# Reordering the products inside each k tile of a decoder layer, so that neighbouring matmuls write different PSUM banks

## The reference, cut to what matters

```python
h = rmsnorm(x, g_mix)
proj = h @ w_in                      # q, k, v, index and gate columns
out_a = dsa_sparse_attention(...)    # 64 of 256 keys by an indexer
out_b = forgetting_attention(...)
mixed = sigmoid(gate_a) * (out_a @ w_o_a) + sigmoid(gate_b) * (out_b @ w_o_b)
x = x + mixed @ w_out
h = rmsnorm(x, g_ffn)
x = x + (silu(h @ w_ffn_gate) * (h @ w_ffn_up)) @ w_ffn_down      # D_FF = 5632
h = rmsnorm(x, g_ple)
x = x + sigmoid(h @ w_ple_gate) * (p @ w_ple_proj)
out = rmsnorm(x, g_final)
```

## Time and profile before

| | |
|---|---|
| runs timed | 1548.62, 1548.97, 1549.17 us |
| median | 1548.97 us |
| span of the profiled execution | 1546.9 us |
| outside of the span (median less span) | 2.1 us |
| TensorE matmul busy | 1516.1 us, 98% of the span |
| mean granted TensorE clock | 0.993 of full speed |
| moved by DMA | 277.56 MB, 179 GB/s |

### The profile page before, as it was taken

The page is one execution under the profiler, slowest core; times in us unless marked ns, Lnnn a source line. Parts: engine busy times, 40 slices in busy tenths (PEclk is TensorE's granted clock), DMA queues, the critical chain, the costliest instruction groups (busy, mean ns, idle before and its releaser), DMA issues.

```text
span 1546.9 us, 25491 instructions
## 1 busy us (share of the span) xinstructions
PE 1516.1 (98%) x8805; PEld 1326.9 (86%) x8805; DVE 986.6 (64%) x1194; ACT 742.2 (48%) x967; POOL 126.4 (8%) x175
## 2 busy tenths in 40 slices
PE   5999999999999999999999999999999999999997
PEld 4888998888988888888888888888888888888886
DVE  6965676667656776766666566556555455555765
ACT  6544435544444664454444444444444444444554
POOL 4011101100111000220000000000000001000031
PEclk8999999999999999999999999999999999999998
DMA  5665475555655555566555655656565565556553
GB/s 140 202 182 174 145 236 164 162 171 177 181 162 163 186 193 182 175 192 188 182 186 176 199 181 182 196 179 188 177 194 174 189 200 177 193 190 198 168 164 109
DMA packets 278124, 277.56 MB, mean 179 GB/s; under 512 B 13048, under 2 KB 275648, under 8 KB 277696
## 3 DMA queue, kind: packets, MB, share of 16 engines
q1 hardware_dynamic: 277632, 275.78, 57.1%
q10 hardware_dynamic: 448, 1.19, 0.2%
HBM read 274.83 MB, written 2.11 MB: 179 GB/s over the span
## 4 chain that ended last, share of the span: by engine, by line
PE 96%; DVE 2%; DMA 1%; ACT 0%; issue 0%; POOL 0%; ACTq 0%; DVEq 0%
PE acc L1178 54%; PE acc L1179 28%; PE acc L1176 3%; PE acc L1175 2%; PE side L1178 2%; PE acc L1280 1%; PE acc L1279 1%; PE acc L1278 1%; PE side L1179 1%; DVE hn L779 1%; DMA rope_c<-in_rope_rows 1%; PE side L1291 0%; PE side L1297 0%; DVE ls L723 0%; PE side L1176 0%
## 5 line engine op out<-in xcount | busy, mean ns | idle before, releaser
L723 DVE TENSOR_TENSOR ls<-ws,hs 128x1024 fp32r<-128x1024 f32 (+2 forms) x528 | 642.9, 1232 | 436.5 <-ACT hs L418 431.9
L418 ACT ACTIVATE hs<-ws 128x1024 fp32r<-128x1024 f32 (+2 forms) x528 | 542.3, 1040 | 535.7 <-PE acc L1179 304.6
L1178 PE MATMUL acc<-xg,hs 128*128 128x512 f32 x1560 | 556.5, 399 | 0.6 <-DVE y_ple L1095 0.6
L1179 PE MATMUL acc<-xg,ls 128*128 128x256 f32 x1560 | 438.1, 281 | 0.0
L1178 PE MATMUL acc<-hn,hs 128*128 128x512 f32 x1005 | 366.4, 406 | 5.8 <-DVE hn L779 5.8
L1178 PEld LDWEIGHTS acc<-xg,hs 128*128 128x128 f32 x1560 | 293.1, 188 | 68.0 <-DVE y_ple L1095 1.0
L1179 PEld LDWEIGHTS acc<-xg,ls 128*128 128x128 f32 x1560 | 294.7, 189 | 5.0
L1179 PE MATMUL acc<-hn,ls 128*128 128x256 f32 x1005 | 283.6, 282 | 0.0
L1178 PE MATMUL acc<-ff,hs 128*128 128x512 f32 x688 | 239.9, 392 | 0.0
L1178 PEld LDWEIGHTS acc<-hn,hs 128*128 128x128 f32 x1005 | 190.5, 190 | 50.9 <-DVE hn L779 7.6
L1179 PEld LDWEIGHTS acc<-hn,ls 128*128 128x128 f32 x1005 | 191.5, 191 | 2.7
(11 more groups left out here) (258 smaller groups left out, 1464.9 us busy)
## 6 DMA issues: line engine op xcount, KB each, us to landing
ws<-in_w_in SPq DMA_DIRECT2D x152, 512.0 KB, 3.7
ws<-in_w_ffn_gate SPq DMA_DIRECT2D x88, 512.0 KB, 4.6
ws<-in_w_ffn_up SPq DMA_DIRECT2D x88, 512.0 KB, 4.4
ws<-in_w_ffn_down SPq DMA_DIRECT2D x64, 512.0 KB, 3.5
ws<-in_w_out SPq DMA_DIRECT2D x32, 512.0 KB, 4.3
ws<-in_w_ple_gate SPq DMA_DIRECT2D x32, 512.0 KB, 4.6
ws<-in_w_ffn_down SPq DMA_DIRECT2D x32, 384.0 KB, 3.6
ws<-in_w_o_b SPq DMA_DIRECT2D x16, 512.0 KB, 3.6
```

The costliest lines, as they stand in the source:

```text
L418: act.activation(hs[:, j, 0:n], ws[:, j, 0:n], ACT.Copy).then_inc(h_split, 1)
L723: dve.tensor_tensor(ls[:, j, 0:n], ws[:, j, 0:n], hs[:, j, 0:n].bitcast(F32), ALU.subtract).then_inc(l_split, 1)
L1178: pe.matmul(whole, *high, start=begins, stop=False)
L1179: mm = pe.matmul(half, *low, start=False, stop=False)
```

## The change

Inside `consume` the loops over rows and k tiles change places: for two rows at a time, and for each k tile, first the high products of both rows, then the low products of both rows. In the last k tile of a unit the two low products come first and then the two high ones. Where only one row is worked on (the first unit, and the last PLE unit), the order is as before. In the PLE projection with its four rows, the rows go two by two.

```diff
-            for m in range(banks) if tile is None else (tile,):
+            rows = range(banks) if tile is None else (tile,)
+            for at_row in range(0, len(rows), 2):
                 for q, k in enumerate(tiles):
-                    at = slice(q * width + m * P, q * width + (m + 1) * P)
                     begins, ends = first and q == 0, last and q == len(tiles) - 1
-                    high, low = (hs[:, j, at], src[:, k, :]), (ls[:, j, at], src[:, k, 0:TOK])
-                    whole, half = acc_of(bank + m, 2 * TOK), acc_of(bank + m, TOK)
-                    if ends:
-                        pe.matmul(half, *low, start=False, stop=False)
-                        mm = pe.matmul(whole, *high, start=False, stop=True)
-                    else:
-                        pe.matmul(whole, *high, start=begins, stop=False)
-                        mm = pe.matmul(half, *low, start=False, stop=False)
+
+                    def whole(m):
+                        at = slice(q * width + m * P, q * width + (m + 1) * P)
+                        return pe.matmul(acc_of(bank + m, 2 * TOK), hs[:, j, at], src[:, k, :], start=begins, stop=ends)
+
+                    def half(m):
+                        at = slice(q * width + m * P, q * width + (m + 1) * P)
+                        return pe.matmul(acc_of(bank + m, TOK), ls[:, j, at], src[:, k, 0:TOK], start=False, stop=False)
+
+                    for part in (half, whole) if ends else (whole, half):
+                        for m in rows[at_row:at_row + 2]:
+                            mm = part(m)
```

## The result

| | before | after |
|---|---|---|
| median | 1548.81 us (1548.62 to 1549.17, 4 runs) | 1536.44 us (1535.77 to 1536.66, 4 runs) |
| span of the profiled execution | 1546.9 us | 1534.6 us |
| TensorE busy | 1516.1 us | 1504.2 us |

The ratio is 0.9919, 95% interval 0.9905 to 0.9933: 12.4 us faster, where 15 us were forecast (1534 us; the range was 1526 to 1550 us). Five later runs of the same kernel gave a median of 1536.56 us.

A forecast was written before the change was run, and what follows sets the result against it. TensorE's distances between matmul starts were taken as the bound. Gains of 16.0 and 0.4 us less 0.8 us lost made 15.6 us, taken as 15: from 1548.97 to 1534 us, range 1526 to 1550 us.

The forecast's parts named there:

- The bound and the kind of cause: Whole kernel: TensorE, 98% busy, sets the time; 33.3 ns per pair lost between products depend on a rhythm of their order.
- the feeders had cover: ScalarE and VectorE splits need 1.06 and 1.25 us within a 2.79 us TensorE chunk, so a faster TensorE costs no waits.
- banks cost nothing: Steps between matmuls: changing or keeping the bank costs nothing in either direction, bounded at 0.01 us a step.
- The pace of H H L L: New order's steady pace: 348.3 ns per pair, from six repeats in the PLE projection; chance 0.60, 1530 to 1539 us.
- lossless: Rival: the new order settles at 346.7 ns per pair, giving 1527 us; chance 0.13.
- columns alone: Rival: distance depends only on the columns streamed, not order, giving 1549 us; chance 0.12, shared with a cancelling mixture of paces.
- The slower rival: Two narrow windows in a row expose weight loads, so the FFN border's 355 ns becomes the steady pace: 1559.5 us; chance 0.15.
- The down groups: Down projection: a group goes from 30.53 to 30.65 us; the seven later groups together lose 0.8 us.
- The sum: Step adding the stages: 16.0 us and 0.4 us gained, 0.8 us lost, 15.6 us together, taken as 15 us.
- the end of a unit: Four narrow and four wide products in a row cost at most 4 x 2 ns, 0.9 us over some 110 ends.
- the six index products: L L L H H H in 1.04 us, 346.7 ns per pair, read as showing that unit ends cost nothing extra.
- 353.3 ns were taken for all 3200 pairs: Old pace assumed over hn, heads_o, mixed and xg; each pair gains 5.0 ns, 16.0 us in all.

The follow-up runs named there:

- e1: Kernel before, each row of a chunk by itself, two k tiles at a time, high high low low into one bank: 1537.18 us, ratio 0.9926.
- e2: Kernel before with the two rows interleaved, widths still alternating (H0 L0 H1 L1 per k tile): 1547.63 us, ratio 0.9995.
- e3: Kernel before with order H0 L1 H1 L0 per k tile, widths still alternating across two banks: 1547.19 us, ratio 0.9991.
- e7: The changed kernel without its low-before-high swap in a unit's last k tile, H0 H1 L0 L1 throughout: 1534.84 us, ratio 0.9912 to the kernel before.
- e10: As e5, but outside the hn stage only every second unit or group has its swaps: 1534.49 us, ratio 0.9909 to the kernel before.
- e6: Kernel before without any swap, high then low for every k tile, the last too: 1551.44 us, ratio 1.0018.
- e5: Kernel before, row 1's low-before-high swap one k tile earlier in a unit's four-tile last chunk: 1535.15 us, ratio 0.9915.
- e4: Kernel before with one more low-before-high swap per unit, in the first chunk, row 0, third k tile: 1538.51 us, ratio 0.9935.

## Why the prediction was right, and where it was off

**The bound and the kind of cause: right, shown.** TensorE's distances between starts set the time, before and after, and the feeders had cover: no wait took the place of the gain. That banks cost nothing was read from the earlier trace rows and is now shown by e1 (all of the gain, no bank change) and by e2 and e3 (bank changes, no gain in the FFN). The change works, but not by what it says of itself.

**The pace of H H L L: right.** 348.3 ns was taken from six quads in the projection. The units of e7 have it exactly; the change has it inside its units. That a figure read from 4.18 us over twelve pairs came out right to 0.1 ns is luck, since 0.01 us in that reading is 0.8 ns per pair; that it was taken from a repeated H H L L and not from single steps isn't. The "lossless" rival (346.7) didn't come about in this order, and "columns alone" is ruled out by e10 and e6 with one order at two paces. The slower rival, the border of the earlier trace rows as a steady state, didn't come about either: inside a unit the quads take 0.69 or 0.70 us, where that border took 0.71. The Trainium skill (TensorE: Matmul & The Clock Gate, "Back-to-back issue gap") gives N / 2.4 + 2.5 ns as the gap of an isolated matmul at the upper clock; an estimate by that figure is 325 ns for this pair, where the fastest took 347 ns. For a stream with a weight load per matmul the Trainium skill (same section) gives about 131 ns at 512 columns instead; the trace doesn't agree, a wide product was followed by the next start after 224 ns at the least.

**The down groups: right.** 30.65 us were foretold, 30.67 measured; the 20 ns between them are the end of a group, priced next.

**What was mis-sized.** The sum came to 15.6 us, cut to 15; the spans differ by 12.3 us. Two terms of the step "The sum" failed. First, the end of a unit (H H L L, L L H H, H H) was put at 8 ns at most. It costs 11.167 us less 11.147 us, 20 ns: over the 110 ends of the sum 2.2 us where 0 to 0.9 us were allowed; e7 gave 1.6 us back by taking it out. Nor are there 110 such ends but 116: a unit over `heads_o` is two sums of eight k tiles, in two pairs of banks, with an end each, and it takes 11.187 us after and 11.147 us in e7, 40 ns apart. The rows used for it, the six index products, have three of a kind and no reversal in front, and were too few to carry it. Second, 353.3 ns were taken for all 3200 pairs, though only `xg` and one unit of `hn` had been read. The timeline of the kernel before has 256 pairs over `heads_o` from the first of these rows to the second:

```profile
501.75 0.48 PE L1178 MATMUL acc<-heads_o,hs 128*128 128x512 f32 x1
...
591.97 0.39 PE L1178 MATMUL acc<-mixed,hs 128*128 128x512 f32 x1
```

90.22 us, 352.4 ns per pair with the slow start included; over `hn`, measured as under e5, the mean was 352.6 ns. There was 0.7 ns less to gain on 1312 pairs, 0.9 us. The two together are the missing 3 us, nearly. The forecast fell within its range because the pace of H H L L, on which most of the sum rests, was read rightly.

## What to carry to other kernels

In a stream in which TensorE never waits, read the distance between starts over tens of matmuls, in every stage, and compare stages with the same instructions: here two paces of one order, 1.8% apart, showed before anything was tried that the time between starts was no constant of the instructions. When a reordering helps, alter each thing that it changed alone, since a same-bank version of this one did the same for 0.7 us more. A place in the old kernel that happens to run the new order for a few repeats gives its steady pace better than a sum of single steps; price the borders between repeats separately.

## What the runs showed of the hardware that was not expected

**Two paces for one order.** Alternating 512- and 256-column products run at 353.3 or 346.9 ns per pair at a granted clock of 1.00, each for hundreds of pairs. Two swaps with two pairs between, at every unit's end, ended in the fast one (e5), in the FFN from the fourth unit on; with three pairs between, the slow one stayed (before). That is no full rule: the down groups of e4, with a third swap two pairs behind these, are slow, and e6 shows both paces without a swap. What brings either pace about, and what in TensorE holds it, is not settled: the traces show starts, and no run here looked inside. The starts do show the slow pace as a pattern of three pairs (distances behind H and L in e6's FFN: 232, 118, 241, 120, 235, 114 ns), and the fast one in e5's FFN as the same pair each time (230 and 117 or 116 ns).

**The loss is one of the upper clock.** While the granted clock was 0.50, the lower level of 1.2 GHz, the same products in the kernel before started 0.43 and 0.21 us apart. The stretch by its granted clock (columns as in the earlier trace rows), and TensorE's timeline in it:

```profile
27.80:29.50 1.70, 1.70 (x7) 1.49 (x6) 1.70 (x3) 0.71 (x2) 0.95 (x1) 0.50 0.33 76
```

```profile
27.87 0.63 PE L1178 MATMUL acc<-hn,hs 128*128 128x512 f32 x1
28.30 0.41 PE L1179 MATMUL acc<-hn,ls 128*128 128x256 f32 x1
28.51 0.63 PE L1178 MATMUL acc<-hn,hs 128*128 128x512 f32 x1
...
29.15 0.63 PE L1178 MATMUL acc<-hn,hs 128*128 128x512 f32 x1
```

Two pairs in 1.28 us, 640 ns per pair, and 768 columns at 1.2 GHz are 640 ns: nothing is lost. At 2.4 GHz, 320 ns, no order of this study lost less than 27 ns per pair over a unit, 13 ns per product. So the orders tried give back 6 of 33 ns, and what holds the other 27 ns wasn't tried.
